# Products with 128 stationary and 64 moving fp32 columns, written as two column halves of the TensorE array

## The reference, cut to what matters

```python
# first mixer, per head, over time
sa = einsum('bhij,bhj->bhi', S, a_t)
S = S * w_t + sa (x) b_t + v_t (x) k_t
y = einsum('bhij,bhj->bhi', S, r_t)
...
# sparse attention: p is the softmax over the selected keys
o = einsum('bthk,btkc->bthc', p, sel) @ w_uv          # per head, 64 values
...
# delta rule, per head and chunk
u = triangular_solve(tri, vb);  w = triangular_solve(tri, kb * exp(gc))
```

## Time and profile before

| | us |
|---|---|
| median of 3 runs | 1429.99 |
| lowest and highest run | 1429.81, 1432.56 |
| the profiled execution (its span; no other time of it is given) | 1434.4 |
| PE busy | 1355.4 |
| weight loads busy | 1114.5 |
| DVE busy | 909.3 |
| ACT busy | 672.5 |
| POOL busy | 217.8 |

### The profile page before, as it was taken

How to read it: one execution, slowest core, us unless ns; L and a number is a source line. 1 busy time by engine, 2 the same in 40 slices (tenths; PEclk the granted TensorE clock), 3 DMA queues, 4 the chain that set the end, 5 groups by cost and what they waited for, 6 DMA issues and landing times. The chain is left out here.

```text
span 1434.4 us, 18474 instructions
## 1 busy us (share of the span) xinstructions
PE 1355.4 (94%) x7272; PEld 1114.5 (78%) x7272; DVE 909.3 (63%) x1255; ACT 672.5 (47%) x964; POOL 217.8 (15%) x123
## 2 busy tenths in 40 slices
PE   6998899999999989999999989989999989989998
PEld 2784569777888877677888868978887879968987
DVE  1686792769778667668665465655455577545664
ACT  2544242255443354546444336554463666326561
POOL 0001432204000041304000000300001342500200
PEclk9999899999999989999999999999999999999999
DMA  8851470267888774555775538824643531118840
GB/s 313 298 198 48 158 254 1 72 191 257 287 307 284 250 203 154 193 176 176 248 222 195 176 111 196 203 88 133 203 140 105 180 130 59 31 57 194 223 144 30
DMA packets 160631, 247.17 MB, mean 172 GB/s; under 512 B 15064, under 2 KB 100028, under 8 KB 160032
## 3 DMA queue, kind: packets, MB, share of 16 engines
q1 hardware_dynamic: 159216, 239.61, 53.0%
q0 software_dynamic: 1328, 6.38, 1.3%
HBM read 244.86 MB, written 4.24 MB: 174 GB/s over the span
## 5 line engine op out<-in xcount | busy, mean ns | idle before, releaser
L199 DVE TENSOR_TENSOR w_lo<-w_raw,w_hi 128x2048 fp32r<-128x2048 f32 (+3 forms) x176 | 403.5, 2299 | 243.9 <-ACT w_hi L190 243.6
L211 PE MATMUL ps<-w_hi,act_hi 128*128 128x512 f32 (+4 forms) x1216 | 473.1, 389 | 17.0 <-DVE act_lo L871 6.4
L212 PE MATMUL ps<-w_lo,act_hi 128*128 128x512 f32 (+4 forms) x1216 | 463.2, 381 | 0.0
L213 PE MATMUL ps<-w_hi,act_lo 128*128 128x512 f32 (+4 forms) x1216 | 462.9, 381 | 0.0
L190 ACT CAST w_hi<-w_raw 128x2048 fp32r<-128x2048 f32 (+3 forms) x176 | 316.9, 1806 | 253.2 <-PE ps L213 210.9
L211 PEld LDWEIGHTS ps<-w_hi,act_hi 128*128 128x128 f32 x1216 | 231.1, 190 | 63.6 <-issue 16.1
L213 PEld LDWEIGHTS ps<-w_hi,act_lo 128*128 128x128 f32 x1216 | 230.8, 190 | 37.5
L212 PEld LDWEIGHTS ps<-w_lo,act_hi 128*128 128x128 f32 x1216 | 231.3, 190 | 33.6 <-issue 0.5
L211 PE MATMUL ps<-w_hi,ffn_gh 128*128 128x512 f32 x176 | 69.7, 396 | 0.0
L678 POOL TENSOR_TENSOR nstat<-nstat,con 128x1 f32<-128x1 f32 x8 | 5.4, 680 | 418.6 <-DVE nstat L673 418.6
L213 PE MATMUL ps<-w_hi,ffn_gl 128*128 128x512 f32 x176 | 68.6, 390 | 0.0
(11 more groups left out here) (508 smaller groups left out, 1817.3 us busy)
## 6 DMA issues: line engine op xcount, KB each, us to landing
w_raw<-in_ffn_w_in SPq DMA_DIRECT2D x88, 512.0 KB, 5.0
w_raw<-in_fox_w_in SPq DMA_DIRECT2D x32, 912.0 KB, 8.0
w_raw<-in_ada_w SPq DMA_DIRECT2D x28, 1024.0 KB, 5.7
w_raw<-in_ffn_w_out SPq DMA_DIRECT2D x20, 1024.0 KB, 5.8
w_raw<-in_rwkv_w_rkv SPq DMA_DIRECT2D x12, 1024.0 KB, 7.7
con<-in_ada_w SPq DMA_DIRECT2D x48, 256.0 KB, 5.4
w_raw<-in_gla_w_in SPq DMA_DIRECT2D x10, 896.0 KB, 4.9
w_raw<-in_gdn_w_in SPq DMA_DIRECT2D x10, 896.0 KB, 4.8
```

The costliest lines, as they stand in the source:

```text
L199: self.nc.vector.tensor_tensor(lo[:, s, 0:c["nk"], 0:c["width"]], self.raw[:, c["slot"], 0:c["nk"], 0:c["width"]], hi[:, s, 0:c["nk"], 0:c ...
L211: nc.tensor.matmul(out(t)[:, 0:w], xh[:, k, tok], hi[:, s, j, 0:w], start=start, stop=False)
L212: nc.tensor.matmul(out(t)[:, 0:w], xh[:, k, tok], lo[:, s, j, 0:w], start=False, stop=False)
L213: return nc.tensor.matmul(out(t)[:, 0:w], xl[:, k, tok], hi[:, s, j, 0:w], start=False, stop=stop)
```

## The change

A helper `column_halves` writes one product as two: stationary columns 0 to 63 with the result in partitions 0 to 63 of `ps`, and stationary columns 64 to 127 with the result in partitions 64 to 127. Both read the same moving operand. Each half occupies half of the array's columns. Changed are `kv`, `ax5`, the first half of `xax5`, `sa` and the 64-column products of `y` in the first mixer, `values` in the attention, and `ax4`, `xax4`, `ax5` in the delta rule. Which products there are, their order, semaphores, buffers and all other engines stay. Per execution 288 products are halved: 64 in `kv`, 32 each in `ax5`, `xax5`, `sa` and `y`, 48 in `values` and 48 in the delta rule.

```diff
+    def column_halves(self, out, lhs, right, start=True, stop=True):
+
+        for c in (0, 64):
+            r = self.nc.tensor.matmul(out[c:c + 64], lhs[:, c:c + 64], right, start=start, stop=stop)
+        return r
...
-                        r = nc.tensor.matmul(ps[:, i, 64 * j:64 * j + 64], kgram[:, j, i, :], m.v[:, t, P * p + 64 * x:P * p + 64 * x + 64],
-                                             start=True, stop=True)
+                        r = core.column_halves(ps[:, i, 64 * j:64 * j + 64], kgram[:, j, i, :], m.v[:, t, P * p + 64 * x:P * p + 64 * x + 64])
...
+            def each_half(q, out, lhs, right, done):
+                for j in range(8):
+                    r = core.column_halves(out(j), lhs(8 * q + j, j), right(8 * q + j, j))
+                r.then_inc(sem(done), 1)
...
-                each(q, lambda j: split(2 + 2 * (q % 2), j), lambda th, j: gram[:, th, 0:P], lambda th, j: blocks3(low[:, th, :]), "ax5")
+                each_half(q, lambda j: split(2 + 2 * (q % 2), j), lambda th, j: gram[:, th, 0:P], lambda th, j: blocks3(low[:, th, :]), "ax5")
...
-                    r = nc.tensor.matmul(ps[:, r_, 64 * j:64 * j + 64], gram[:, 8 * q + j, P:2 * P], mm.sa[r_][:, 64 * j:64 * j + 64],
-                                         start=not t, stop=not t or j % 2 == 1)
+                    r = core.column_halves(ps[:, r_, 64 * j:64 * j + 64], gram[:, 8 * q + j, P:2 * P], mm.sa[r_][:, 64 * j:64 * j + 64],
+                                           not t, not t or j % 2 == 1)
...
-                    r = nc.tensor.matmul(out(n)[:, j * 64:j * 64 + 64], pt[:, n % 2, b, j, :], vh[:, b, (4 * g + j) * 64:(4 * g + j) * 64 + 64],
-                                         start=(b == 0), stop=(b == t))
+                    r = core.column_halves(out(n)[:, j * 64:j * 64 + 64], pt[:, n % 2, b, j, :], vh[:, b, (4 * g + j) * 64:(4 * g + j) * 64 + 64],
+                                           b == 0, b == t)
```

More of the change, by code:

```diff
@@ L1841, in xax5 @@
                 x = mm.x[q % 2]
-                each(q, lambda j: ps[:, 3 + 2 * (q % 2), 64 * j:64 * j + 64], lambda th, j: up[:, th, :], lambda th, j: x[:, j, :], "low5_mm")
+                each_half(q, lambda j: ps[:, 3 + 2 * (q % 2), 64 * j:64 * j + 64], lambda th, j: up[:, th, :], lambda th, j: x[:, j, :], "low5_mm")
                 each(q, lambda j: split(2 + 2 * (q % 2), j, 64), lambda th, j: x[:, j, :], lambda th, j: odd(up[:, th, :]), "up5_mm")
@@ L1868, in sa @@
                     pe.wait_ge(sem("rhs"), r_ + 1)
-                each(q, lambda j: ps[:, r_, 64 * j:64 * j + 64], lambda th, j: up[:, th, :],
-                     lambda th, j: rhs[t][:, r_ * COLS + 64 * j:r_ * COLS + 64 * j + 64], "sa_mm")
+                each_half(q, lambda j: ps[:, r_, 64 * j:64 * j + 64], lambda th, j: up[:, th, :],
+                          lambda th, j: rhs[t][:, r_ * COLS + 64 * j:r_ * COLS + 64 * j + 64], "sa_mm")
             def y(q):
@@ L3636, in each, with each_half @@
             r.then_inc(sem("g_" + done), 1)
+        def each_half(q, out, lhs, right, done):
+            for h in range(VH):
+                r = core.column_halves(out(h), lhs(VH * q + h, h), right(VH * q + h, h))
+            r.then_inc(sem("g_" + done), 1)
         def split(b, h, n=P):
@@ L3655, in ax4 @@
         def ax4(q):
-            each(q, lambda h: ps[:, 2 + 2 * q, 64 * h:64 * h + 64].rearrange("p (m s) -> p m s", s=16), lambda th, h: am[:, th, :],
-                 lambda th, h: up[:, th, :].rearrange("p (m two s) -> p m two s", two=2, s=16)[:, :, 1, :], "ax4")
+            each_half(q, lambda h: ps[:, 2 + 2 * q, 64 * h:64 * h + 64].rearrange("p (m s) -> p m s", s=16), lambda th, h: am[:, th, :],
+                      lambda th, h: up[:, th, :].rearrange("p (m two s) -> p m two s", two=2, s=16)[:, :, 1, :], "ax4")
         def xax4(q):
@@ L3661, in xax4 @@
             pe.wait_ge(sem("g_low4"), q + 1)
-            each(q, lambda h: ps[:, 3 + 2 * q, 64 * h:64 * h + 64], lambda th, h: mm.low4[:, th, :], lambda th, h: mm.x[q][:, h, :], "up4_mm")
+            each_half(q, lambda h: ps[:, 3 + 2 * q, 64 * h:64 * h + 64], lambda th, h: mm.low4[:, th, :], lambda th, h: mm.x[q][:, h, :], "up4_mm")
         def ax5(q):
             pe.wait_ge(sem("g_up4"), 4 * q + 4)
-            each(q, lambda h: split(2 + 2 * q, h), lambda th, h: am[:, th, :], lambda th, h: odd(up[:, th, :]), "ax5")
+            each_half(q, lambda h: split(2 + 2 * q, h), lambda th, h: am[:, th, :], lambda th, h: odd(up[:, th, :]), "ax5")
         def xax5(q):
```

## The result

The changed kernel takes 1410.59 us (median of 4 runs, 1408.06 to 1412.03) against 1431.12 for the one before beside it: ratio 0.9848, 95% interval 0.9823 to 0.9874. Run again later beside ten runs of before it took 1411.06 against 1430.03, ratio 0.9871 (0.985 to 0.9892). So it is 19 to 20.5 us faster, where 17.3 were forecast; both are inside the range.

What follows compares the result with a forecast made beforehand. PE, busy 94% of the span, was taken to set the pace; gains counted only where PE is waited for, 1.2 + 3.1 + 7.3 + 0 + 2.3 + 3.4 = 17.3 us, gave a median of 1412.7 us, range 1408 to 1422.

Steps and rivals of the forecast that it cites:

- The price of a halved product: All changed places: 0.117 us instead of 0.224 if halves overlap, 0.107 saved; 0.009 lost if they do not.
- The estimate of 1430 us: Whole kernel: by the skill's warning on small dimensions, 64 moving columns leave little to win, sum about 1430.
- place 2: First mixer, ax5 and xax5 of the first tile, 32 products: 3.1 us saved.
- place 3: First mixer, ax5, sa, xax5 and y from 236.95 to 253.81, 64 products: 7.3 us saved.
- place 4: First mixer, sa and y of the second tile, 32 products: counts 0, since DVE is busy throughout.
- place 5: Attention, 48 products: 2.3 us saved, partly limited by ACT's exponentials and DVE's slack.
- place 6: Delta rule, 48 products: 3.4 us saved, after new division changes (0.9) and two new waits (0.8).
- the two waits: Delta rule: xax4(1) for ACT's second copy into low (about 0.3), turn_up for DVE's four copies (0.5).
- place 1: kv, 64 products: PE gains 6.8 us, but turn_up(0) waits for DVE's transposes, so 1.2 us counted.
- B: Rival: half the gain, from loads hindering each other or new waits; about 8 us, 1422; chance 0.11.
- C: Rival: no overlap of the short pairs, slower, 1433.6 us; chance 0.07.
- D: Rival: more, DVE gives way too in kv or at the first mixer's end, up to 5 us, 1408; chance 0.05.

Runs made afterwards that it cites:

- Experiment 1: Changed kernel with the two halves of each group's products written one after the other, not alternating, in first mixer and delta rule: 1421.18 us, ratio to before 0.9939.
- experiment 5: Four kernels, halves at one place only, rest as before: kv 1430.99, doubling 1420.88, attention 1426.70, delta rule 1428.60 us, against before's 1430.76.
- experiment 3: Changed kernel with the state products of the first mixer's second tile halved too: 1411.73 us, ratio to before 0.987.

## Why the prediction was right

**The price of a halved product.** Forecast 0.117 us (-0.107), measured 0.119. Experiment 1 shows that the alternation makes it. The estimate of 1430 us, from 64 moving columns being few, did not come about: what was split are the 128 stationary columns, and a product fell from 0.224 us to 0.119. The Trainium skill (TensorEngine Tiling (Array Packing), Key Properties) says that tiles operate independently, loads and matmuls in parallel; the trace agrees, with 30 ns a pair where one half alone has 58.

**Place by place.** *Doubling, first tile* (place 2): `turn_up(0)` to `ax5(2)` took 236.95 - 218.50 = 18.45 and takes 227.00 - 211.52 = 15.48, -3.0, forecast -3.1. *From `ax5(2)` on* (place 3): -7.4, forecast -7.3. *Second tile* (place 4): 0.0 for DVE, forecast 0; the statement that `y` takes PE as long as before was wrong by 0.13 us a pair of heads, without effect. *Attention* (place 5): -1.9, forecast -2.3; ACT's exponentials remain its longest wait, with 1.64 us. *Delta rule* (place 6): 9.80 - 13.15 = -3.35, forecast -3.4. That it fits so well is in part luck: the two waits come to about 0.5 us instead of 0.8, and so the changes of division cost some 1.2, as an estimate (48 x 0.105 - 0.5 - 3.35), not 0.9.

**Kv** (place 1) is the step that failed. Its sign, `turn_up(0)` within 0.3 us of the transposes' end, is not in the trace of the changed kernel: it is 1.9 us there, behind a loop that a transfer and the clock had held up. Where the wait is for DVE (experiment 5), the 1.2 us are there, and are lost again to a clock that the prediction had named as a danger for other stretches, the attention and the delta rule, and not for this one, where it had itself worked out that PE would wait. It had looked at the wait as a length only. The price is 1.3 to 2.6 us in the six traces that have it. The 1.2 us themselves came from one trace: in the five traces with whole kv `turn_up(0)` starts 0.9 to 3.5 us after the transposes' end.

**The rest of the gain.** The places sum to 15.6, the single kernels to 16.0, and the whole is 19 to 20.5. Of the difference some 2.5 us are in stretches that the change does not touch: 840-863 and 1250-1285 in the table are shorter where the attention is in halves (the second not in the kernel without kv). The second is a wait for a weight transfer. PE at 1288 us in before, and in the changed kernel:

```profile
1287.97 1.09 PE L639 MATMUL ps<-con,x_res 128*128 128x128 f32 x8 [1.42 <-DVE x_res L594]
```
```profile
1262.41 1.09 PE L645 MATMUL ps<-con,x_res 128*128 128x128 f32 x8
```

DVE was late because its cast weights were, and the cast (ACT, L190) had waited 5.84 us for their transfer in before and 4.24 in the changed kernel; why the transfers land better after a shorter attention was not tested. With these 2.5 us the places come to some 18. The remainder, 1 to 2.5 us, is not larger than the uncertainty of the two ratios, and its cause is open; the 3.1 us of the column 146-157 may have a part in it, if runs of before lack them more often than others, which one trace of before cannot show. So the total is near the forecast partly by luck: kv's 1.2 us and 0.4 of the attention did not come, and 3 to 5 us came that no place had in its sum.

**The rivals.** B (half the gain) would have shown groups of 1.36 us for 8 products, and they take 0.96. C (no overlap) is excluded by the same rows. D asked for more than the places give, and the median did come out 1.6 to 2.1 us below the forecast, though not in kv or at the mixer's end, where D had put it.

## What to carry to other kernels

Here a product with 128 stationary and 64 moving fp32 columns was bound by its weight load (112 ns a pair, 58 with 64 stationary columns); written as two column halves in turn it takes about half the time, 0.119 us for 0.224. That holds as long as the neighbours use that division too (0.09 to 0.17 us for each change of it). With more moving columns it ends: the state products of experiment 3, with 128, took 0.22 us in halves, no less than the 0.224 of whole ones by the pace of the earlier trace rows. Alternate the halves pair by pair. Then count only where PE is what the others wait for, and where it is not, look at whether the new wait is long enough to cost the clock: 3.5 to 5.7 us of idleness ahead of a short group nearly doubled that group's time (1.06 us became 1.88 to 1.97).

## What the runs showed of the hardware

- Across a seam between two halves PE overlaps about three pairs (experiment 1: 16 products in 3.05 us, 1.91 in turn, 3.7 without overlap), so halves in runs of 16 pairs lose most of the overlap, not all.
- With four quarters a pair starts each 14 ns, and a product takes 0.114 us, nearly the same as with two (0.119).
- In the densest stretch of quarters, 128 pairs in 1.8 us, 1.52 and 0.88 us passed between two starts in which PE waited for no semaphore.
- The clock was at the lower level after waits of 3.5 to 5.7 us, and a group of eight transposes took 1.97 us instead of 1.06. A wait of 2.37 us ended at full clock, which fell 2 us later. In the kv loop waits of 2.53 and 2.16 us were followed by the lower clock as well (0.50 from 198 to 202 us in the first).
